# ScalarE's order of work in the scan of a hybrid block, and at the first attention head

## The reference

```python
z, xbc, dt_raw, q, k, v, f_raw = jnp.split(h @ w_in, SPLITS)
xbc = silu(causal_depthwise_conv(xbc, conv_w, conv_b))      # xs, B, C
# ssd_chunked, per chunk of 128
decay_in = exp(segsum(a))                                   # matrix per head, 128 x 128
scores = (C @ B^T) * decay_in
y_diag = scores @ (xs * dt)
states = B^T @ (xs * dt * exp(a_cs[-1] - a_cs))
y_off = (C @ prev_states) * exp(a_cs)
y_ssm = rms_norm((y + d_skip * xs) * silu(z), ssm_norm_w)
# forgetting_attention, per head
probs = softmax(q @ k^T * scale + cum_t - cum_s, causal)
```

## Time and profile before

| | |
|---|---|
| median of 3 runs | 1512.77 us (1512.42 to 1517.89) |
| profiled execution, its own time | 1512.18 us |
| its span | 1510.4 us |
| PE busy | 1433.1 us, 95% of the span |
| DVE, ACT, POOL busy | 685.8, 513.9, 653.2 us |

### The profile page before, as it was taken

The page is one execution under the profiler, slowest core; times in us unless marked ns, Lnnn a source line. Parts: engine busy times, 40 slices in busy tenths (PEclk is TensorE's granted clock), DMA queues, the critical chain, the costliest instruction groups (busy, mean ns, idle before and its releaser), DMA issues.

```text
span 1510.4 us, 17544 instructions
## 1 busy us (share of the span) xinstructions
PE 1433.1 (95%) x6751; PEld 1178.5 (78%) x6751; DVE 685.8 (45%) x1013; ACT 513.9 (34%) x738; POOL 653.2 (43%) x518
## 2 busy tenths in 40 slices
PE   2998999999999979999999997979998999999999
PEld 2886788788888868888888876867887888888887
DVE  6674765479852875131221366236623313122131
ACT  0634343344444443132322324323434313232231
POOL 1541254444232765445454553552134444445452
PEclk9997999999999989999999998999999999999999
DMA  9241334453432423232323231311012232322322
GB/s 332 93 141 58 110 121 160 138 177 120 161 101 84 142 57 110 91 104 87 108 84 110 83 114 57 109 56 56 29 57 74 93 104 91 97 98 91 104 83 83
DMA packets 119991, 157.38 MB, mean 104 GB/s; under 512 B 5196, under 2 KB 81248, under 8 KB 119936
## 3 DMA queue, kind: packets, MB, share of 16 engines
q1 hardware_dynamic: 117744, 151.15, 31.0%
q0 software_dynamic: 1648, 5.39, 1.1%
q10 hardware_dynamic: 544, 0.10, 0.0%
HBM read 154.45 MB, written 2.17 MB: 104 GB/s over the span
## 4 chain that ended last, share of the span: by engine, by line
PE 85%; DVE 6%; POOL 4%; ACT 2%; issue 2%; DMA 1%; SPq 0%; POOLq 0%; DVEq 0%; ACTq 0%
PE bank L1426 24%; PE bank L1428 24%; PE bank L1427 24%; PE bank L1563 3%; POOL w_lo L484 2%; PE bank L1758 2%; PE bank L1553 2%; PE bank L1890 1%; DVE tmp L1012 1%; PE bank L1538 1%; DMA arena<-in_w_ada_dram 1%; POOL head_rs L468 1%; PE bank L1678 1%; PE bank L1528 1%; DVE early L1129 1%
## 5 line engine op out<-in xcount | busy, mean ns | idle before, releaser
L484 POOL TENSOR_TENSOR w_lo<-raw,w_hi 128x512 fp32r<-128x512 f32 x428 | 579.7, 1387 | 658.2 <-ACT w_hi L615 658.1
L1426 PE MATMUL bank<-w_hi,a_hi 128*128 128x512 f32 x928 | 365.4, 394 | 4.5 <-DVE a_lo L932 3.5
L1427 PE MATMUL bank<-w_lo,a_hi 128*128 128x512 f32 x928 | 363.4, 392 | 0.0
L1428 PE MATMUL bank<-w_hi,a_lo 128*128 128x512 f32 x928 | 363.3, 392 | 0.0
L1426 PE MATMUL bank<-a_hi,w_hi 128*128 128x512 f32 x800 | 318.0, 397 | 17.3 <-POOL w_lo L484 15.6
L615 ACT ACTIVATE w_hi<-raw 128x2048 fp32r<-128x2048 f32 x107 | 204.7, 1913 | 366.5 <-PE bank L1428 362.6
L1428 PE MATMUL bank<-a_hi,w_lo 128*128 128x512 f32 x800 | 314.0, 392 | 0.0
L1427 PE MATMUL bank<-a_lo,w_hi 128*128 128x512 f32 x800 | 313.9, 392 | 0.0
L1426 PEld LDWEIGHTS bank<-w_hi,a_hi 128*128 128x128 f32 x928 | 175.8, 189 | 41.7 <-DVE a_lo L932 3.7
L1428 PEld LDWEIGHTS bank<-w_hi,a_lo 128*128 128x128 f32 x928 | 175.5, 189 | 36.9
L1427 PEld LDWEIGHTS bank<-w_lo,a_hi 128*128 128x128 f32 x928 | 175.6, 189 | 36.0
(11 more groups left out here) (218 smaller groups left out, 1182.5 us busy)
## 6 DMA issues: line engine op xcount, KB each, us to landing
raw<-in_w_in_dram SPq DMA_DIRECT2D x32, 1024.0 KB, 5.3
raw<-in_w_mlp_dram SPq DMA_DIRECT2D x32, 1024.0 KB, 5.2
arena<-in_w_ada_dram SPq DMA_DIRECT2D x18, 1024.0 KB, 5.4
raw<-in_w_ff_in_dram SPq DMA_DIRECT2D x16, 1024.0 KB, 5.3
raw<-in_w_ff_out_dram SPq DMA_DIRECT2D x16, 1024.0 KB, 5.0
raw<-in_w_out_dram SPq DMA_DIRECT2D x12, 1024.0 KB, 5.1
arena<-in_w_ada_dram SPq DMA_DIRECT2D x3, 2048.0 KB, 18.0
early<-acs_d SPq DMA_DIRECT2D x4, 1024.0 KB, 9.6
```

Source lines behind the costliest of these rows:

```text
L484: last = pool.tensor_tensor(w_lo[:, u0 % 2, cols], raw[:, u0 % 2, cols], w_hi[:, u0 % 2, cols].bitcast(F32), ALU.subtract)
L1426: pe.matmul(out_, hi_a, hi_b, start=start, stop=False)
L1427: pe.matmul(out_, hi_a, lo_b, start=False, stop=False)
L1428: return pe.matmul(out_, lo_a, hi_b, start=False, stop=stop)
```

## The change

Three things move, all on ACT; no instruction is added or taken away, except that a table of functions may be loaded at another place.

- Copies 2 and 3 go behind tap 10 and Silu 9, instead of behind tap 11, `hi` of unit 8 and Silu 10. `hi` of unit 8 goes behind Silu 10. Copies 4 and 5 go ahead of Silu 11.
- The decays are cut in two, `small_decays` (three small exponentials) and `decay_matrix`. Those of chunk 0 stand ahead of copies 6 to 9, those of chunk 2 between `hi` of unit 9 and `hi` of unit 10, ahead of the reading of z(1).
- At s = 1 of the attention the exponentials of head 0 go ahead of the reading of that step's tile.

```diff
-            def decays(ch):
+            def small_decays(ch):
                 e, b = ex2[:, ch % 2], bc[:, ch % 2]
                 act.wait_ge(dta_made, 1)
...
                 act.activation(e[:, 2], e[:, 2], ACT.Exp).then_inc(ex_made, 1)
+
+            def decay_matrix(ch):
                 act.wait_ge(bc_sub, ch + 1)
-                act.activation(b, b, ACT.Exp).then_inc(bc_exp, 1)
+                act.activation(bc[:, ch % 2], bc[:, ch % 2], ACT.Exp).then_inc(bc_exp, 1)
...
-                if n % 2:
+                if n % 2 and n < CT - 1:
                     hi(U_XBC + n // 2 + 2)
                 if n:
                     conv_silu(n - 1)
                 if n == 6:
                     copy_xs(0)
                     copy_xs(1)
-                elif n == 11:
+                elif n == 10:
                     copy_xs(2)
                     copy_xs(3)
-            conv_silu(CT - 1)
+            hi(U_Z + 1)
             copy_xs(4)
             copy_xs(5)
+            conv_silu(CT - 1)
+            small_decays(0)
             for m in range(6, 10):
                 copy_xs(m)
-            decays(0)
+            decay_matrix(0)
             read_z(0)
-            decays(1)
+            small_decays(1)
+            decay_matrix(1)
             hi(U_Z + 2, late=1)
+            small_decays(2)
             hi(U_Z + 3)
             read_z(1)
-            decays(2)
+            decay_matrix(2)
             read_z(2)
-            decays(3)
+            small_decays(3)
+            decay_matrix(3)
...
-                if s < 12:
+                if s < 12 and s != 1:
                     if s % 2 == 0:
                         hi(U_QK1 + s // 2 + 1)
                     qk_tile(s // 4 + 1, s % 4, U_QK1 + 2 * (s // 4), s % 2)
                 if 1 <= s < 17:
                     h = s - 1
                     probabilities(h, lambda q: prob[:, h % 2, QO[q]:QO[q] + (q + 1) * P], prob[:, h % 2])
-                if s == 14:
+                if s == 1:
+                    qk_tile(1, 1, U_QK1, 1)
+                elif s == 14:
                     hi(U_WO1 + 2, late=1)
```

## The result

| | before | after |
|---|---|---|
| median | 1514.86 us (4 runs, 1512.42 to 1517.89) | 1497.99 us (4 runs, 1496.99 to 1500.49) |
| ratio | | 0.9892, 95% interval 0.9867 to 0.9918 |
| profiled execution | 1512.18, span 1510.4 | 1498.39, span 1496.6 |

The kernel is 1.1% faster, and the time lies 0.5 us from the 1498.5 that was forecast. The profiled spans differ by 13.8 us, against 14.3 in the sum. The medians differ by more, 16.9 us, since that of the kernel before is 1514.86 us here and was 1512.77 when the forecast was made. The terms of that sum were not all right: one was priced 2 us too high, and a loss of 3.2 us that the sum doesn't have took its place.

What follows compares the result with a forecast made beforehand. PE, with 85% of the chain of waits, was taken as the bound. 12.4 us by chunk 2's end plus 1.9 at the head made 14.3 off: 1498.5 us on the median of 1512.77, range 1494 to 1503.

Steps and rivals of the forecast that it cites:

- Turns 4 and 5: Scan start: early copies let PE's turns follow conv tile 11 at 116.23, so turn 6 starts at 122.6 instead of 128.03.
- Small exponentials, table load: Ahead of copies 6 to 9: DVE starts chunk 0's matrix at 122.63, taking 1.76 us from table load to DVE's start.
- First collision: DVE's matrix 0 and POOL's `w_lo` of unit 8 take turns; z(0,1) starts at 126.75, 1.9 us after it could.
- Chunk 0 and 1: Scan: chunk 0 at full clock ends at 137.7, 11.8 us won; chunk 1 ends at 155.7, 12.9 us early.
- Chunk 2: Scan: a new 2.0 us wait for unit 10's `w_lo` replaces 1.31; chunk 2 ends at 175.9, 12.4 us won.
- Head: First attention head: exponentials ahead of the tile's reading remove PE's wait before the first turn of probabilities, 1.93 us won.
- I take 0 for the rest: Behind chunk 2 every wait keeps its distance from that chunk's end, so nothing more is won or lost.
- (C): Rival: a new gap of about 2 us drops the clock, 1.6 us each, two make 3.2; 1500 to 1502 us; chance 0.18.
- (B): Rival: collisions cost less, by other interleaving or z(2,1) finding unit 10 ready; without both waits 1494.6 us; chance 0.17.
- (D): Rival: clock stays low after both gaps, costing 12.2 us; 2 us of gain remain, 1510.6, no difference; chance 0.06.
- (E): Rival: slower, clock falls at 124.9 and stays at 0.50 through the scan; all of it would give 1545; chance 0.04.
- A: The forecast as summed, 14.3 us off; own range 1496.5 to 1500.5 us; chance 0.55.

Runs made afterwards that it cites:

- copies_only: Kernel before with only the early copies and the moved conversion of unit 8, decays left whole; median 1514.79 us against 1515.31, ratio 0.9982.
- small0_late: Changed kernel with the small exponentials of chunk 0 moved back behind copies 6 to 9; median 1503.78 us, ratio 0.9919 to the kernel before.
- two_steps: Changed kernel with `w_lo` of unit 8 made in two of four POOL steps, the other half left out; median 1493.98 us, ratio 0.9863 to the kernel before.
- dve_lo8: Changed kernel with `w_lo` of unit 8 made by idle DVE, all but its last 32 columns; median 1495.44 us, ratio 0.9860 to the kernel before.
- small2_late: Changed kernel with the small exponentials of chunk 2 moved back behind the reading of z(1); median 1503.39 us, ratio 0.9932 to the kernel before.
- scan_only: Changed kernel with the edit at the first attention head taken back; median 1500.71 us, ratio 0.9893 to the kernel before.
- head_only: Kernel before with the edit at the first attention head alone; median 1510.31 us against 1515.36, ratio 0.9972.
- after_again: The changed kernel unaltered, run once more on the same chip as the others; median 1499.22 us, ratio 0.9887 to the kernel before.
- spread_sums: Changed kernel with the 16 column sums ahead of the first logits split, 8 at s = 0 and 8 at s = 1; median 1499.46 us, ratio 0.9883.
- one_each: Changed kernel with one pair of column sums per attention step, the last four pairs at s = 12 and 13; median 1499.63 us, ratio 0.9894.
- dve_lo8_each: Changed kernel with the edits of dve_lo8 and one_each together; median 1496.98 us, ratio 0.9874 to the kernel before.

## Why the prediction was right

**Turns 4 and 5, first low clock.** As worked out: the turns follow tile 11, turn 6 starts at 122.17 (122.6 in the sum; this execution runs 0.4 us ahead from the turns on). But copies_only shows that of the 5.9 us won here little is left by themselves, 2.7 us in its timed runs.

**Small exponentials, table load.** DVE at 122.41, 122.63 forecast. The table load started at 120.64 and took 1.28 us, and the first exponential started at 121.93. The Trainium skill (ScalarE: Activation LUTs, What ACT_TABLE_LOAD costs) gives 2.66 us for a switch; this trace shows 1.29, so the row was the better base.

**First collision.** The gap of 1.9 us ahead of z(0,1) measured 1.67, and `w_lo` of unit 8 took 7.06 us where 4.97 + 2.3 were forecast. The question that was left between 0 and 1.24, whether the minimum of line 1130 is held too, is answered: 2.17 instead of 1.23 us, so 0.94. Chunk 0's products end at 137.34 (137.7). The Trainium skill (GPSIMD Engine Reference, Key points) names contention with DVE instructions that have two SBUF inputs or run in a 2-port mode. This trace agrees for the two inputs of line 1138 (2.74 instead of 2.29 us). Line 1139 has one and was held too; no row says in which mode it ran. The runs small0_late, two_steps and dve_lo8 show the collision as the cause of the gap.

**Chunk 0 and 1.** Full clock in chunk 0: state product and 32 products take 5.4 us instead of 10.5, as forecast. DVE starts matrix 1 at 135.01 (135.15), chunk 1 ends at 155.27 (155.7).

**Chunk 2, the term that was wrong.** The sum had a wait of 2.0 to 2.1 us for `w_lo` of unit 10, with bounds of 0 and 2.1, and took the upper end. Measured is next to none: PE was busy 8.97 of the 9 us from 156 to 165. It was close: POOL's last step ended at 160.79 and z(2,1) began at 160.84, 0.2 us after its turn. The step that failed is the 8.2 us of DVE work that were put on POOL's 8 x 1.24. POOL needed 15.82 us, so it was held 5.9. The four of its eight steps that took longer than 1.3 us, the last of the DVE instructions in question, and the weight load of PE (PEld) that waited for POOL's last step, each from its engine's timeline:

```profile
144.97 3.09 POOL L484 TENSOR_TENSOR w_lo<-raw,w_hi 128x512 fp32r<-128x512 f32 x1 [18.70 <-ACT w_hi L615]
149.27 3.32 POOL L484 TENSOR_TENSOR w_lo<-raw,w_hi 128x512 fp32r<-128x512 f32 x1
152.56 2.24 POOL L484 TENSOR_TENSOR w_lo<-raw,w_hi 128x512 fp32r<-128x512 f32 x1
157.27 2.28 POOL L484 TENSOR_TENSOR w_lo<-raw,w_hi 128x512 fp32r<-128x512 f32 x1
```

```profile
159.63 2.25 DVE L1176 TENSOR_TENSOR arena<-arena,ex 128x1024 f32<-128x1024 f32 x1
160.84 0.19 PEld L1435 LDWEIGHTS bank<-w_hi,a_hi 128*128 128x128 f32 x1 [0.45 <-POOL w_lo L484]
```

Every DVE instruction had been counted in full, but one that finds a POOL step under way waits itself for the rest of it. Against POOL's 1.24 us a step, the instructions of 2.29 us added 1.9 (the rest of line 1160) and 2.1 us, and two of those of 1.23 us added 1.0 each. The third of these, line 1167 of before (1176 here), waited for POOL's last step (2.25 us) and held nobody. That one is the largest part of the difference. So chunk 2 ended at 173.5, not 175.9, and 14.7 us were won there instead of 12.4; 0.4 of that was there already at the end of chunk 1. The old wait of 1.31 us is gone by the step named: small2_late brings it back, larger.

**Head.** 1.93 us forecast; 1.9 in scan_only's gap and in head_only's mark.

**Behind chunk 2, "I take 0 for the rest".** Wrong by 3.2 us in the profiled execution: 14.7 + 1.9 = 16.6 were due at the first turn of probabilities, 13.5 were there, and the stretch of 7.6 us at 0.55 is what lies between. No rival had this: (C) put falls of the clock behind new gaps, and behind the gap of 1.67 us it stayed at 1.00, in all six executions that have it. It fell where PE had no gap at all. The argument against (C), that the clock stays up behind a gap of 1.93 us, was true of the one trace it was read from: in scan_only and copies_only it fell there. So that (C) didn't occur is not a rule.

So the forecast of 14.3 us met 13.8 by an error of 2.3 too little and one of 3.2 too much, with 0.3 more won behind it. That the two nearly cancel is luck, and so is the 0.5 us between the medians: the one forecast started from a median 2.1 us below that of the result. The rivals: (B) had the right end for z(2,1) and the wrong one for z(0,1); (D) and (E) did not occur. What tells A from luck in the mechanism is the list of marks up to chunk 1, each within 0.5 us.

**Open.** What decides whether the clock falls in a stretch of full busy time is not settled. At the first logits it was seen in after, after_again, scan_only, copies_only, small2_late, two_steps and spread_sums, and not in before, head_only, small0_late, dve_lo8, one_each and dve_lo8_each. The last two have four sums there instead of 16. The head's edit does not explain it, and the column sums ahead of the logits explain where it can come, not whether it does.

## What to carry to other kernels

An engine's idle gap is worth more than its length where PE's clock falls behind it, and moving the gap forward (copies_only) brings little; find the small instructions that let the slowest follower start earlier, here three exponentials of 16 columns, and put those ahead. When work of DVE moves in time, look at what POOL does in the new place: two engines that hold each other take turns, so count for each only what goes beyond the other's turn, and look whether the one that waits anyway can do the other's work. And a fraction of a per cent in one profiled execution may be the clock of that execution.

## What the runs showed of the hardware

- The granted clock fell to 0.50 (1.2 GHz) in stretches in which PE was busy without a break, for 3.4 to 6.9 us, and not at the same places in the two executions of the changed kernel. The products ahead of it were small ones: 128x1 sums and 64-row logits (1.84 and 3.96 us). In after_again and copies_only it also fell within 32 products of 64 columns that stand behind a gap of 0.75 us (4.90 us in after_again instead of some 3.7); in the eleven other executions it did not.
- A gap of PE of 3.05 us had low clock behind it in copies_only and small0_late, one of 2.38 us in small2_late for some 3 us. A gap of 1.93 us had none in the kernel before; the same gap in scan_only (1.94) and copies_only (1.93) had low clock for 3.4 us. One of 1.67 us had none in six executions.
- A DVE instruction with one input (line 1130, 2048 elements in 1.23 us) is held by POOL like one with two: 2.17 to 2.20 us in three places.
- One DVE subtraction of 128x2016 took 2.26 us; all 2048 columns on POOL in four steps took 7.06 us with DVE in between and 5.01 without (small0_late).
